# Rows of squares added by DMAs, two rows for squares, one root for two norms, sums of inputs later

## The reference, cut to what matters

```python
def rmsnorm(x, g):
    y = x * lax.rsqrt(mean(x * x, axis=-1, keepdims=True) + EPS)   # EPS 1e-5 in block 1, 1e-6 in block 2
    return y * g

# block 1
x = x + mix(rmsnorm(x, norm1_g)) @ w_out
h2 = rmsnorm(x, norm2_g)                               # norm "n2"
x = x + (silu(h2 @ w_gate) * (h2 @ w_up)) @ w_down
x = rmsnorm(x, normf_g)                                # norm "nf", and at once
# block 2
p = rmsnorm(x, g_attn_2) @ w_in_2                      # a second norm of the same rows
...
x = x + concat([y_a, y_b, y_c]) @ w_out_2
h2 = rmsnorm(x, g_ffn_2)                               # norm "n3"
x = x + square(relu(h2 @ w_ff1_2)) @ w_ff2_2
return rmsnorm(x, g_final_2)                           # norm "fin"
```

## Time and profile before

| | |
|---|---|
| time, median of 3 runs | 2557.63 us (2556.87 to 2558.29) |
| the profiled execution's own time | 2557.67 us |
| its span, first to last instruction | 2555.9 us |
| mean granted clock of TensorE | 0.983 of 2.4 GHz |
| PE busy | 2436.8 us, 95% |
| DVE busy | 1755.1 us, 69% |
| ACT busy | 999.0 us, 39% |
| POOL busy | 1029.4 us, 40% |

### The profile page before, as it was taken

One profiled execution on the slowest core, in us unless ns is written; L12 is line 12 of the kernel. 1 busy time (PEld: TensorE's weight loads), 2 busy tenths in 40 slices (PEclk: granted clock), 3 DMA queues, 4 the chain that ended last, 5 costly groups with the idle time before them and its releaser, 6 DMA issues.

```text
span 2555.9 us, 30901 instructions
## 1 busy us (share of the span) xinstructions
PE 2436.8 (95%) x11502; PEld 1991.5 (78%) x11502; DVE 1755.1 (69%) x2401; ACT 999.0 (39%) x1700; POOL 1029.4 (40%) x692
## 2 busy tenths in 40 slices
PE   8899999999889999999998988999989999999996
PEld 6667788878678888888886866887868888888884
DVE  6776667673877677676766998777396566666664
ACT  5455655552533222232243125555252232322332
POOL 3756542211534444444452342331253343433333
PEclk9999999999999999999999999999999999999997
DMA  4312221132111111112122222222211111212111
GB/s 148 79 46 56 86 58 46 53 113 72 45 38 58 54 50 50 58 54 58 46 58 81 72 67 59 58 71 92 78 46 46 54 54 46 58 45 59 49 51 70
DMA packets 149204, 158.65 MB, mean 62 GB/s; under 512 B 10304, under 2 KB 108352, under 8 KB 148928
## 3 DMA queue, kind: packets, MB, share of 16 engines
q1 hardware_dynamic: 149056, 156.67, 20.4%
HBM read 122.55 MB, written 15.20 MB: 54 GB/s over the span
## 4 chain that ended last, share of the span: by engine, by line
PE 83%; DVE 9%; ACT 3%; issue 2%; POOL 1%; DMA 1%; SPq 0%; POOLq 0%; DVEq 0%; ACTq 0%
PE PS L1516 24%; PE PS L1521 24%; PE PS L1518 23%; PE PS L1580 3%; PE PS L1567 2%; PE PS L1601 2%; PE PS L1598 2%; PE PS L1561 2%; DVE R L1859 1%; DVE R L1876 1%; PE PS L1564 1%; DVE Pb L1751 1%; DVE sm L1737 1%; DVE Pb L1749 1%; DVE X L1820 1%
## 5 line engine op out<-in xcount | busy, mean ns | idle before, releaser
L1516 PE MATMUL PS<-R,wh 128*128 128x512 f32 x2952 | 1170.2, 396 | 22.5 <-DVE stage L1673 8.0
L1521 PE MATMUL PS<-R,wh 128*128 128x512 f32 x2952 | 1157.5, 392 | 14.3 <-DVE R L1876 14.2
L2215 POOL TENSOR_TENSOR lows<-values,wh 128x512 fp32r<-128x512 f32 (+1 forms) x420 | 610.2, 1456 | 1116.7 <-ACT wh L2023 1011.6
L1518 PE MATMUL PS<-R,lows 128*128 128x512 f32 x2588 | 1014.9, 392 | 1.1 <-POOL lows L2215 1.1
L1521 PEld LDWEIGHTS PS<-R,wh 128*128 128x128 f32 x2952 | 557.7, 189 | 137.6 <-DVE R L1876 18.1
L1516 PEld LDWEIGHTS PS<-R,wh 128*128 128x128 f32 x2952 | 559.1, 189 | 134.6 <-DVE stage L1673 8.8
L1518 PEld LDWEIGHTS PS<-R,lows 128*128 128x128 f32 x2588 | 490.1, 189 | 97.4 <-issue 2.4
L2023 ACT ACTIVATE wh<-values 128x512 fp32r<-128x512 f32 (+1 forms) x420 | 261.8, 625 | 762.4 <-PE PS L1521 704.0
L1863 DVE TENSOR_TENSOR X<-PS,X 128x512 f32<-128x512 f32 x400 | 273.0, 691 | 248.4 <-PE PS L1521 248.4
L1840 DVE TENSOR_TENSOR stage<-PS,stage 128x512 f32<-128x512 f32 x153 | 104.1, 688 | 102.5 <-PE PS L1521 102.3
L2215 POOL TENSOR_TENSOR late_r<-late,wh 128x512 fp32r<-128x512 f32 x72 | 108.2, 1504 | 135.8 <-ACT wh L2023 96.6
(11 more groups left out here) (251 smaller groups left out, 2714.2 us busy)
## 6 DMA issues: line engine op xcount, KB each, us to landing
values<-w_in_dram SPq DMA_DIRECT2D x92, 256.0 KB, 2.8
values<-w_ff_dram SPq DMA_DIRECT2D x92, 256.0 KB, 2.9
R<-R SPq DMA_DIRECT2D x96, 128.0 KB, 2.3
values<-w_down_dram SPq DMA_DIRECT2D x40, 256.0 KB, 2.8
late<-w_ff_dram SPq DMA_DIRECT2D x36, 256.0 KB, 3.0
values<-w_up_dram SPq DMA_DIRECT2D x35, 256.0 KB, 3.0
values<-w_gate_dram SPq DMA_DIRECT2D x32, 256.0 KB, 3.0
values<-w_out_dram SPq DMA_DIRECT2D x20, 256.0 KB, 2.8
```

The source lines that it names most:

```text
L1516: e.matmul(PS[:, b, :], wh, high, start=s["start"], stop=False)
L1518: e.matmul(PS[:, b, :], wl, high, start=False, stop=False)
L1521: m = e.matmul(PS[:, b, :], wh, low, start=False, stop=s["stop"])
L2215: e.tensor_tensor(T.wl[piece.v][:, 0:m], T.wv[piece.v][:, 0:m], T.wh[:, piece.h, 0:m].bitcast(F), ALU.subtract).then_inc(*sg.up("w_lo", pi ...
```

## The change

It makes five edits:

- GpSimd no longer adds a row of squares to `mix`. It issues a DMA from the row of squares to `mix` that adds to its target, and whose landing is the event `acc2`. The planner prices it at 1.0 us on GpSimd, its bytes at 300 GB/s and a latency of 1.8 us.
- In norm nf squares go to two rows in turn, and squares with the gain to two others (`T.squares` rows 1, 3, 5, 7). n2, n3 and fin keep the one row `P2`.
- In nf and fin the last row (e = 7) is squared by halves and not added to `mix`. `rs_sum` becomes two matmuls for each half, `mix` and then the last row, into one bank.
- One root for two norms: the second norm's mean is made of both sums, still in their banks, so its root is the whole `rstd`. L1669, L1671 and `rstd_both` go.
- The first pair of each feed-forward block runs P1, P2, P3, P6, P5, P7, P4. P3's bank is held until S65 is made, and P7 and P4 get banks 0 and 1. `right_sum`, `right_hi` and `right_lo` have `later` 110 instead of 60.

The diff, cut to its core:

```diff
@@ about
     if engine == "gpsimd":
+        if op == "dma_start":
+            return 1000.0
         return 150 + 2.4 * n
@@ dense_seven
+        sums_late = names[1] == "P2"
-        for name in ("P1", "P6", "P2", "P5", "P7", "P3", "P4"):
+        for name in names:
-            b = self.seven_at % 3
+            b = dict(P7=0, P4=1).get(name, self.seven_at % 3) if sums_late else self.seven_at % 3
             self.seven_at += 1
             elif name == "P2":
-                self.bank_given[b] = [add("C11", name, "a", "a", ["S1", "S6"])]
-                evac("C11", None, stage["a"], [], ("seven", (t, "C11")))
+                to = "e" if sums_late else "a"
+                self.bank_given[b] = [add("C11", name, to, "a", ["S1"] if sums_late else ["S1", "S6"])]
+                evac("C11", None, stage[to], [], ("seven", (t, "C11")))
+            elif name == "P3" and sums_late:
+                held = b
             elif name == "P5":
                 self.bank_given[b] = [add("S65", name, "c", "b", ["S6"])]
+                if sums_late:
+                    b = held
+                    self.bank_given[b] = [add("C12", "P3", "a", "c", ["S65", "S6", "C11"])]
+                    evac("C12", None, stage["a"], [], ("seven", (t, "C12")))
@@ rsqrt
         for half, (b, given, i, gi, j, gj) in enumerate(halves):
-            self.step("rs_sum", n=n, half=half, src=src, waits=list(waits), b=b, given=given)
-            self.step("rs_mean", n=n, half=half, dim=dim, eps=eps, extra=extra, extra_waits=list(extra_waits), b=b, i=i, gi=gi)
+            self.step("rs_sum", n=n, half=half, src=src, waits=list(waits), last=last, b=b, given=given)
+        for half, (b, given, i, gi, j, gj) in enumerate(halves):
+            self.step("rs_mean", n=n, half=half, dim=dim, eps=eps, over=over, b=b, i=i, gi=gi)
@@
+SEVEN_FIRST = ("P1", "P2", "P3", "P6", "P5", "P7", "P4")
@@ post_x
-        p2 = [] if e < 2 else [("accg_sum", (name, e - 1)) if g2_col is not None else ("acc2", (name, e - 1))]
-        O.step("post_square", name=name, e=e, done=list(done), first=list(first), p2=p2)
-        if g2_col is not None:
-            O.step("post_gain", name=name, e=e, done=list(done), first=list(first), g2_col=g2_col)
+        before = 2 if name == "nf" else 1
+        free = [("acc2", (name, e - before))] if e > before else []
+        gain_free = [("accg_sum", (name, e - 2))] if e > 2 else []
+        for half in range(2) if e == 7 and name in ("nf", "fin") else [None]:
+            mine = list(done) if half is None else [done[half]]
+            O.step("post_square", name=name, e=e, half=half, done=mine, first=list(first), free=free)
+            if g2_col is not None:
+                O.step("post_gain", name=name, e=e, half=half, done=mine, first=list(first), g2_col=g2_col, free=gain_free)
@@ right_sums (the same for right_hi and right_lo)
-            O.step("right_sum", tag=tag, j=j, a=a, gcol=gcol, given=x + freed, later=60)
+            O.step("right_sum", tag=tag, j=j, a=a, gcol=gcol, given=x + freed, later=110)
@@ second_norm
-        tr1 = O.rsqrt("mix", S, EPS1, "r1", [("acc2", ("nf", 7)), ("accg_sum", ("nf", 7))])
-        tr2 = O.rsqrt("rstd", S, EPS2, "mix", [("accg_sum", ("nf", 7))], extra=True, extra_waits=tr1)
-        O.step("rstd_both", waits=tr2)
-        O.rstd_ready = [("rstd_both", 0)]
+        tr1 = O.rsqrt("mix", S, EPS1, "r1", [("acc2", ("nf", 6))], last=("square", [("sq2", ("nf", 7, half)) for half in range(2)]))
+        O.rstd_ready = O.rsqrt("rstd", S, EPS2, "rstd", [("accg_sum", ("nf", 6))], over=(*O.sums_in, EPS1),
+                               last=("gained", [("sqg", ("nf", 7, half)) for half in range(2)]))
@@ tensor_program, rs_sum
-            e.matmul(PS[:, s["b"], :], T.ones[:, :], T.rows[s["src"]][:, cols(half)], start=True, stop=True).then_inc(*sg.up("rs_sum", (s["n"], half)))
+            last = s["last"]
+            m = e.matmul(PS[:, s["b"], :], T.ones[:, :], T.rows[s["src"]][:, cols(half)], start=True, stop=not last)
+            if last:
+                row, events = last
+                w.wait_ge(*sg.at(*events[half]))
+                m = e.matmul(PS[:, s["b"], :], T.ones[:, :], T.rows[row][:, cols(half)], start=False, stop=True)
+            m.then_inc(*sg.up("rs_sum", (s["n"], half)))
@@ vector_program, rs_mean
-                e.tensor_tensor(va, PS[:, b, :], r1, ALU.mult).then_inc(*sg.up("rs_part", (key, half, 0)))
+                e.tensor_scalar(va, PS[:, banks[half], :], -0.5 * eps / dim, -0.5 * eps * first_eps, ALU.mult, ALU.add).then_inc(
+                    *sg.up("rs_part", (key, half, 0)))
...
+                e.scalar_tensor_tensor(va, PS[:, b, :], -0.5 / dim, va, ALU.mult, ALU.add).then_inc(*sg.up("rs_mean", (key, half)))
@@
+def square_row(T, name, k):
+    return T.squares[:, 1 + 2 * (k % 2), :] if name == "nf" else T.P2[:, 0:S]
@@ gpsimd_program
-        elif kind == "post_square" and s["e"]:
+        elif kind == "post_square" and s["e"] and s["half"] is None:
             name, k = s["name"], s["e"]
             w.wait_ge(*sg.at("sq2", (name, k)))
             w.wait_ge(*(sg.at("acc0", name) if k == 1 else sg.at("acc2", (name, k - 1))))
-            e.tensor_tensor(T.mix[:, :], T.mix[:, :], T.P2[:, 0:S], ALU.add).then_inc(*sg.up("acc2", (name, k)))
+            e.dma_start(T.mix[:, :], square_row(T, name, k), accum_op=ALU.add).then_inc(*sg.up("acc2", (name, k), by=16))
```

More of the change, by code:

```diff
@@ L191, in __init__ @@
         self.lamc = self.sm[:, 0:1]
-        self.rows = dict(mix=self.mix, rstd=self.rstd, r1=self.P2[:, 0:S], CV5=self.CV[5], CV6=self.CV[6])
+        self.rows = dict(mix=self.mix, rstd=self.rstd, r1=self.P2[:, 0:S], P2=self.P2, square=self.squares[:, 3, :], gained=self.squares[:, 7, :], CV5=self.CV[5], CV6=self.CV[6])
     def at(self, name, shape, dt, offset):
@@ L586, in dense_last, with rsqrt @@
                         self.split_piece()
-    def rsqrt(self, src, dim, eps, dst, waits, extra=False, extra_waits=(), banks=None, stages=None):
+    def rsqrt(self, src, dim, eps, dst, waits, over=None, last=None, banks=None, stages=None):
         if len(self.dense_banks) == 8:
@@ L1155, in right_sums @@
         for a in (0, 1, 2, 3):
[L1156 removed]
+            O.step("right_sum", tag=tag, j=j, a=a, gcol=gcol, given=x + freed, later=110)
         for a in (1, 0, 2, 3):
[L1158 to L1159 removed]
+            O.step("right_hi", tag=tag, j=j, a=a, later=110)
+            O.step("right_lo", tag=tag, j=j, a=a, later=110)
     def second_pass(name, tag, src, src_ready, xp, xp_done, dst, gcol, freed, ready):
@@ L1196, in start_ffn, with make_rstd @@
         O.lend_stages(MIDDLE, O.rstd_ready)
-    def make_rstd(dim, eps, acc):
-        O.rstd_ready = O.rsqrt("mix", dim, eps, "rstd", [acc] + O.rstd_ready)
+    def make_rstd(dim, eps, name):
+        O.rstd_ready = O.rsqrt("mix", dim, eps, "rstd", [("acc2", (name, 6))] + O.rstd_ready,
+                               last=("P2", [("sq2", (name, 7, half)) for half in range(2)]))
     def hidden_free(tag, t):
@@ L1479, in work_order @@
     assert O.used == len(O.turns)
-    make_rstd(S, EPS2, ("acc2", ("fin", 7)))
+    make_rstd(S, EPS2, "fin")
     for half in range(2):
@@ L1871, in vector_program @@
                     w.wait_ge(*sg.at("accg_sum", (name, k - 1)))
-                e.tensor_tensor(rstd[:, :], rstd[:, :], T.P2[:, 0:S], ALU.add).then_inc(*sg.up("accg_sum", (name, k)))
+                e.tensor_tensor(rstd[:, :], rstd[:, :], T.squares[:, 5 + 2 * (k % 2), :], ALU.add).then_inc(*sg.up("accg_sum", (name, k)))
         elif kind == "post_lo":
@@ L1920, in vector_program @@
                 *sg.up("hid_lo", key))
-        elif kind == "rstd_both":
-            for event in s["waits"]:
-                w.wait_ge(*sg.at(*event))
-            e.tensor_tensor(rstd[:, :], T.mix[:, :], T.rows["r1"], ALU.mult).then_inc(*sg.up("rstd_both", 0))
         elif kind == "x2_out":
@@ L2163, in scalar_program @@
                 e.activation(T.rstd[:, :], x, ACT.Square, scale=gain2).then_inc(*sg.up("accg", (name, 0)))
-            else:
-                w.wait_ge(*sg.at("acc2", (name, k)))
-                e.activation(T.P2[:, 0:S], x, ACT.Square, scale=gain2).then_inc(*sg.up("sqg", (name, k)))
+            elif s["half"] is None:
+                for event in s["free"]:
+                    w.wait_ge(*sg.at(*event))
+                e.activation(T.squares[:, 5 + 2 * (k % 2), :], x, ACT.Square, scale=gain2).then_inc(*sg.up("sqg", (name, k)))
+            else:
+                cc = cols(s["half"])
+                for event in s["free"]:
+                    w.wait_ge(*sg.at(*event))
+                e.activation(T.squares[:, 5 + 2 * (k % 2), cc], x[:, cc], ACT.Square, scale=gain2).then_inc(*sg.up("sqg", (name, k, s["half"])))
         elif kind == "gate_evac":
@@ L2422, in engine_orders @@
             assert event not in given, event
-            given[event] = end + LATENCY[engine]
```

(1 more changed line is left out.)

37 lines of the change are left out of this document (19 added, 18 removed).

## The result

The changed kernel takes 2552.56 us (median of 13 runs, 2551.19 to 2554.26), the kernel before 2557.63 (13 runs beside it, 2555.88 to 2561.36): a ratio of 0.998, 95% interval 0.9972 to 0.9989. That is 5 us gained where 23.7 were forecast. The profiled execution has a span of 2551.1 us, that of before 2555.9.

A forecast was written before the change was run, and what follows sets the result against it. TensorE bounds the kernel, with losses at three norm seams and the end. Gains of 12.4 (seam 1), 5.3 (seam 3), 11.5 (seam 2), 0.5 (end), less charges of 4 and 2, made 23.7 us: 2534 us, range 2517 to 2568.

The forecast's parts named there:

- L: Chains of adding DMAs in the norms: time from a square's end to its DMA's landing, taken at 4.6 us.
- two bounds: Limits for an adding DMA's time: 2.7 us (plain 512 KB transfer) to 8.1 us (two transfers and a GpSimd issue).
- The tail in seam 1: Norm n2, last add to P1: 11 us for sums, roots, VectorE steps, plus 4 for evacuations freeing bank 0.
- Seam 3: Norm n3: TensorE resumes 5.3 us earlier, at most 9; some 8 us of today's wait laid to right_sum/right_lo.
- The relief of VectorE: Seam 1 (n2): VectorE regains time lost beside GpSimd's adds, at most 15 us, taken as 10.
- The 4 us for blocked ScalarE and GpSimd queues: Seams 1 and 3: loss from instructions queued behind DMA waits, 0.3 us a step over 14 steps.
- The 2 us for banks: Two seams: second pair's P1 waits for an evacuation of bank 1, which P4 filled; 2 us lost.
- Seam 2: Norm nf: two rows and one root remove stalls and half clock; rs_sum near 1350, net 11.5 us gained.
- rival (c): Adding DMAs of in-between speed, 5.2 to 5.9 us each: 2545 to 2562 us; chance 0.17.
- price for an L of 5.5: Whole kernel, under the slower-DMA rival: 5 us gained if an adding DMA takes 5.5 us.
- rival (d): Seams 1 and 3 don't gain, VectorE stays full or sums precede evacuations: 2548 us; chance 0.08.
- Rival (a): Adding DMAs fast, 4.2 us or below, so TensorE bounds the seams: 2520 us; chance 0.22.

The follow-up runs named there:

- e12: Changed kernel with DMAs that overwrite mix instead of adding to it (plain DMAs, norms of last rows only); 2536.6 us.
- e13: Changed kernel with the products' PSUM banks turned by one, so P1 of n2's first pair takes bank 2, freed first; 2550.9 us.
- e15: Kernel before with only the new order of the first pair's products and the later right-hand sums; 2552.9 us.
- e10: Changed kernel plus two square rows in n2, n3, fin; last row of n2, n3 summed by TensorE; no bank clash; weight buffers given back at the sums; 2528.5 us.
- e11: e10 with the adds of squares as GpSimd instructions again; 2535.4 us.
- e1: Changed kernel with the adds of squares as GpSimd instructions again, all else as changed; 2541.7 us.

## Why the prediction was wrong, step by step

Two terms of the sum failed. L, taken at 4.6 us, measured 5.39 in n2 and 5.30 in n3; and the way from the last landing to P1, taken at 15 us in seam 1, measured 22.5. A third step, that some 8 us of seam 3 were `right_sum` and `right_lo` on the path, had the wait itself wrong.

**L, the time of an adding DMA.** Mis-sized. I took 4.6 us. From the end of the square to landing it is 4.83 where nothing else moves (fin), 5.39 in the mean of n2's seven (4.8 to 6.3) and 5.30 in n3. The formula around it was right: with 5.39, 662.5 + 7L is 700.2, and the last DMA landed at 699.5. In n3 and at the end the first squares end within 0.2 us of where the forecast had them, once the shift of the earlier stages is taken off, and last landings are late by 4.5 us in n3 (7 x 0.70 = 4.9) and 1.5 at the end (6 x 0.23 = 1.4). The rest of a step was 1.08 us, not 1.15, which gives a little back. So this term cost 4.8 us in seam 1 (699.5 against 694.7), 4.5 in seam 3 and 1.5 of the 2.0 at the end, where five of the eight sums, at half clock, took some more. Of the forecast's two bounds L lies nearer to the lower one, 2.7 us. The Trainium skill ("DMA: Bandwidth & Descriptors", Anatomy of one DMA) gives 3.2 us for the plain DMA, by estimate, and e12 shows 3.2 from the end of the square and 2.9 from the issue. The second source read that the Trainium skill ("Collectives: The Full Stack", The bandwidth ceiling) has for an add made the estimate 4.4; measured 4.83 undisturbed.

**The tail in seam 1.** Mis-sized, and the larger miss. From the last add to P1 I had 11 + 4 = 15 us; it is 22.5. To the written norm it takes 13.1, mostly since TensorE came out of its stand at half clock (0.50) and the four sums took 3.8 us instead of 2.0; from there to bank 0 it takes 9.4, not 4 (e13). I had counted one or two evacuations; bank 0 is freed by the seventh. 4.8 + 7.5 = 12.3 us later than forecast, 722.0 instead of 709.7. Less the charge of 2 us that wasn't needed, and with the 0.4 us by which the stages before seam 1 were faster, this is 10.7 of the 10.6 that seam 1 missed.

**Seam 3.** The step "some 8 us are right_sum/right_lo" was wrong: no one waited for them there (e15: +1.2 us, its wait at P7 included). The tail of n3 is 19.7 us, not 17. 4.5 + 2.7 + 1 (banks) - 2 (charge) = 6.2 of the 6.3 that seam 3 missed.

**The relief of VectorE.** It is there: seven of the eight `post_lo` (L1902) of n2 take 1.27 to 1.28 us and one 2.10, where four took 2.3 to 3.35 before, and TensorE's stalls behind it are gone. The 10 us that I took for seam 1 were not priced by a run of their own: e10 against e11 holds the relief of GpSimd's queue too, and e10 still stands 3.36 us for its chain.

**The charges.** The 4 us for blocked ScalarE and GpSimd queues were not needed: in neither seam of the changed kernel does TensorE wait over 0.5 us for a weight's high or low part. The 2 us for banks were there, one of the two for another pair of products.

**Seam 2.** Right in mechanism and size: 12.0 us gained, 11.5 forecast, and rs_sum at 1351.09 (1350.2 on the clock of the kernel before; "near 1350"):

```profile
1351.09 1.12 PE L1557 MATMUL PS<-mix,ones 128*128 128x512 f32 x2 [0.45 <-DMA mix<-SQ]
```

The granted clock of that stretch is 1.00, where it was 0.90.

**The rivals.** What happened is rival (c), L of 5.2 to 5.9 with 2545 to 2562 us, which had a chance of 0.17; the stated range, 2517 to 2568 us, holds the measured time. That the forecast's own price for an L of 5.5, 5 us gained, is what came is luck: with the L of each norm its sum gives 12 us, the longer tails take 10.2 of them, and the 4 us that were charged for nothing come back, with smaller terms of both signs. Of rival (d) seam 3 has the outcome, no gain, but not the cause: VectorE was not full there (41.88 of 50 us), and no one had waited for the sums. Rival (a) was wrong in its price: the plain DMA of e12 has such an L, and came out at 2536.6, not 2520, since the tail stays and ScalarE's queue keeps the chain from getting shorter by 7L.

## What to carry to other kernels

A step moved off a vector engine into a serial chain of DMAs pays each DMA's full latency, here 4.8 to 6.3 us against 2.7 for the instruction; before anything else give the chain a second source buffer and end it one link earlier. Both together, with the clash of banks gone on either side, turned a loss of 11 us against the GpSimd adds (e1) into a gain of 7 (e10 against e11). And when a wait before the bound engine is to go, count the instructions of the whole queue up to the event that it waits for, bank by bank: two of my three misses were in what stands behind the chain, not in the chain.

## What the runs showed of the hardware

**An adding DMA and a weight load slow each other.** All six adding DMAs of fin, with no load beside them, land 4.52 to 4.54 us after issue. In n2 the rows of three short stretches of the changed kernel (the DMAs issued in them) show one with no load beside it, one with one and one with two:

```profile
mix<-P POOLq DMA_DIRECT2D x1, 512.0 KB, 4.5
...
mix<-P POOLq DMA_DIRECT2D x1, 512.0 KB, 6.0
values<-w_gate_dram SPq DMA_DIRECT2D x1, 256.0 KB, 3.5
...
values<-w_up_dram SPq DMA_DIRECT2D x2, 256.0 KB, 4.2
mix<-P POOLq DMA_DIRECT2D x1, 512.0 KB, 5.5
```

In n2 the three with no load under way take 4.52 to 4.56 us and the four with one or two loads of 256 KB 4.9 to 6.0; such a load takes up to 5.4 us, against 3.1 at most beside the plain DMAs of e12. That is where L's mean of 5.39 comes from.

**The issue costs GpSimd 0.88 us** per adding DMA, 0.57 per plain one of the same size (e12), and 0.3 to 0.4 us pass between the end of the square and its start where it waits for the square alone.
